# Cross attention: the values made in token layout, without transposes

## The reference

```python
def cross_attention(xn, mem_n, w_q, w_kv, w_o):
    q = (xn @ w_q).reshape(b, s, X_HEADS, X_HEAD_DIM)        # 4 heads of 256
    kv = mem_n @ w_kv
    k = kv[..., :X_HEADS * X_HEAD_DIM].reshape(b, -1, X_HEADS, X_HEAD_DIM)
    v = kv[..., X_HEADS * X_HEAD_DIM:].reshape(b, -1, X_HEADS, X_HEAD_DIM)
    logits = jnp.einsum('bshd,bmhd->bhsm', q, k).astype(jnp.float32) * X_HEAD_DIM ** -0.5
    p = jax.nn.softmax(logits, axis=-1)
    o = jnp.einsum('bhsm,bmhd->bshd', p.astype(v.dtype), v).reshape(b, s, X_HEADS * X_HEAD_DIM)
    return o @ w_o
```

## Time and profile before

| what | value |
|---|---|
| median of three runs | 1918.83 us (1918.15 to 1919.11) |
| profiled execution | 1919.41 us, its span 1917.6 us |
| PE busy | 1893.5 us, 99% of the span |
| POOL busy | 1393.7 us, 73% |
| DVE busy | 943.0 us, 49% |
| ACT busy | 546.1 us, 28% |

### The profile page before, as it was taken

The page is one execution under the profiler, slowest core; times in us unless marked ns, Lnnn a source line. Parts: engine busy times, 40 slices in busy tenths (PEclk is TensorE's granted clock), DMA queues, the critical chain, the costliest instruction groups (busy, mean ns, idle before and its releaser), DMA issues.

```text
span 1917.6 us, 23896 instructions
## 1 busy us (share of the span) xinstructions
PE 1893.5 (99%) x8875; PEld 1564.7 (82%) x8875; DVE 943.0 (49%) x1500; ACT 546.1 (28%) x1093; POOL 1393.7 (73%) x1646
## 2 busy tenths in 40 slices
PE   9999999999999999999999999999999999999997
PEld 7777788888888888888888888888799888888886
DVE  5888788752442212135776664333744643122124
ACT  5666644431120102022345551111322311010012
POOL 6555479998887777778644657777898777777773
PEclk9999999999999999999999999999999999999999
DMA  5222123333333333333322323332433233333321
GB/s 169 78 77 69 48 80 94 96 110 114 95 99 99 94 95 97 99 99 89 87 56 67 88 67 94 99 99 86 126 111 110 81 98 99 99 99 96 92 83 60
DMA packets 341319, 177.43 MB, mean 93 GB/s; under 512 B 14470, under 2 KB 338220, under 8 KB 341205
## 3 DMA queue, kind: packets, MB, share of 16 engines
q1 hardware_dynamic: 338978, 173.14, 31.5%
q10 hardware_dynamic: 2226, 2.76, 0.6%
HBM read 173.75 MB, written 2.13 MB: 92 GB/s over the span
## 4 chain that ended last, share of the span: by engine, by line
PE 93%; DVE 4%; ACT 2%; issue 1%; DVEq 0%; POOL 0%; POOLq 0%; ACTq 0%
PE bank L678 27%; PE bank L680 27%; PE bank L682 27%; PE bank L814 2%; PE bank L766 1%; PE bank L1050 1%; PE bank L1051 1%; PE bank L1052 1%; DVE fQS L1808 1%; PE bank L746 1%; PE bank L792 1%; PE bank L1116 1%; PE bank L1136 1%; PE bank L777 1%; PE bank L862 0%
## 5 line engine op out<-in xcount | busy, mean ns | idle before, releaser
L617 POOL TENSOR_TENSOR WL<-RAW,WH 128x256 fp32r<-128x256 f32 (+2 forms) x1276 | 1031.2, 838 | 29.2
L611 POOL TENSOR_SCALAR WH<-RAW 128x1024 fp32r<-128x1024 f32 (+3 forms) x331 | 354.6, 1071 | 465.0 <-PE bank L682 413.7
L678 PE MATMUL bank<-HH,WH 128*128 128x512 f32 x1560 | 619.0, 397 | 0.5 <-DVE HL L1754 0.5
L682 PE MATMUL bank<-HH,WL 128*128 128x512 f32 x1560 | 615.4, 394 | 0.0
L680 PE MATMUL bank<-HL,WH 128*128 128x512 f32 x1560 | 610.3, 391 | 0.0
L678 PEld LDWEIGHTS bank<-HH,WH 128*128 128x128 f32 x1560 | 293.3, 188 | 60.6 <-issue 6.3
L682 PEld LDWEIGHTS bank<-HH,WL 128*128 128x128 f32 x1560 | 293.0, 188 | 59.4 <-issue 1.9
L680 PEld LDWEIGHTS bank<-HL,WH 128*128 128x128 f32 x1560 | 293.3, 188 | 58.2 <-issue 3.1
L2012 DVE TENSOR_TENSOR X<-X,bank 128x512 f32<-128x512 f32 x80 | 55.0, 687 | 234.1 <-PE bank L682 234.1
L678 PE MATMUL bank<-UH,WH 128*128 128x512 f32 x256 | 99.6, 389 | 0.0
L680 PE MATMUL bank<-UL,WH 128*128 128x512 f32 x256 | 99.6, 389 | 0.0
(11 more groups left out here) (408 smaller groups left out, 2996.8 us busy)
## 6 DMA issues: line engine op xcount, KB each, us to landing
RAW<-in_w_in SPq DMA_DIRECT2D x107, 512.0 KB, 3.6
RAW<-in_w_up SPq DMA_DIRECT2D x32, 512.0 KB, 3.9
RAW<-in_w_down SPq DMA_DIRECT2D x32, 512.0 KB, 3.9
RAW<-in_w_ffn_gate SPq DMA_DIRECT2D x22, 512.0 KB, 3.7
RAW<-in_w_ffn_up SPq DMA_DIRECT2D x22, 512.0 KB, 3.7
RAW<-in_w_xkv SPq DMA_DIRECT2D x16, 512.0 KB, 3.8
RAW<-in_w_ffn_down SPq DMA_DIRECT2D x16, 512.0 KB, 3.9
RAW<-in_w_proj_attn SPq DMA_DIRECT2D x8, 512.0 KB, 3.9
```

Of the source, the lines that this page charges most:

```text
L611: nc.gpsimd.tensor_scalar(WH[:, s, 0:k, :], RAW[:, s, 0:k, :], 1.0, 1.0, ALU.mult, ALU.mult).then_inc(S_[f"hi_made{s}"], 1)
L617: nc.gpsimd.tensor_tensor(WL[:, s, own_tiles, :], RAW[:, s, own_tiles, :], WH[:, s, own_tiles, :].bitcast(F32), ALU.subtract).then_inc(S_[ ...
L678: mm(psum[s][:, 0:n], WH[:, s, k, :], hi(k), start=(k == 0), stop=False)
L682: last = mm(psum[s][:, 0:n], WL[:, s, k, :], hi(k), start=False, stop=(k == tiles - 1))
```

## The change

The values are made with memory tokens on the partitions at once. The memory is the stationary operand (a block of 128 features by 128 tokens), and 256 weight columns of a head move. A unit of the values is now 512 rows by 256 columns, in the same slot and of the same size; both units of a head add into one bank, two blocks of tokens side by side. The transposes and `XV` go. The norm of a token is then one number per partition: two further products with one column give the sums of squares per partition (`RMEM`), ACT takes their root and DVE the reciprocal, and ACT and DVE multiply by it where they make the halves. The bank of a head's values stays taken until then.

```diff
-        XQ, XK, XV = sb("XQ", [P, 2, S]), sb("XK", [P, 2, MEM]), sb("XV", [P, 2, MEM])
+        XQ, XK = sb("XQ", [P, 2, S]), sb("XK", [P, 2, MEM])
...
+        def of_pair(tile, s):
+            return tile[:, s, :, :].rearrange("p (k c) n -> p k (c n)", c=2)
...
+            def load_pair(name, it, j, src):
+                s, c = units.use(name, it, j)
+                sp.wait_ge(S_[f"unit_cut{s}"], 4 * c - 4)
+                sp.dma_start(of_pair(RAW, s), src.rearrange("(k p) n -> p k n", p=P)).then_inc(S_[f"landed{s}"], 16)
...
-                for j in range(4):
-                    load("cross", h, 2 + j, cols(w["w_xkv_2"], h * 2 * P + (D * (j // 2) + P * (j % 2))))
+                for j in range(2):
+                    load("cross", h, 2 + j, cols(w["w_xkv_2"], h * 2 * P + P * j))
+                for j in range(2):
+                    load_pair("cross", h, 4 + j, w["w_xkv_2"][bass.ds(j * D // 2, D // 2), bass.ds(D + h * 2 * P, 2 * P)])
...
-            mm(OUTB[:, 0:MEM], ones[:], ACCM[:], start=True, stop=True).then_inc(once("mem_stat")[0], 1)
+            mm(OUTB[:, 0:MEM], ones[:], ACCM[:], start=True, stop=True)
+            for mb in range(MEM // P):
+                last = mm(OUTB[:, MEM + mb:MEM + mb + 1], ACCM[:, mb * P:(mb + 1) * P], ones[:, 0:1],
+                          start=True, stop=True)
+            last.then_inc(once("mem_stat")[0], 1)
...
-            for j in range(4):
+            def mem_values(h):
+                bank_slot, bank_use = units.use("cross", h, 5)
+                bank = psum[bank_slot]
+                pe.wait_ge(S_[f"taken{bank_slot}"], bank_use - 1)
+                for half in range(2):
+                    s, c = units.use("cross", h, 4 + half)
+                    for k in range(4):
+                        pe.wait_ge(S_[f"unit_cut{s}"], 4 * c - 3 + k)
+                        for mb in range(MEM // P):
+                            for v, weight in ((0, WH), (0, WL), (1, WH)):
+                                last = mm(bank[:, mb * 2 * P:(mb + 1) * 2 * P],
+                                          MEMC[v][:, 4 * half + k, mb * P:(mb + 1) * P], of_pair(weight, s)[:, k, :],
+                                          start=(half == k == mb == v == 0 and weight is WH),
+                                          stop=(half == 1 and k == 3 and v == 1), skip_group_check=True)
+                                if k == 3 and mb == 1 and v == 1:
+                                    last.then_inc(S_[f"product{s}"], 1)
+                                yield
+
+            for j in range(2):
                 run(from_mem(0, 2 + j))
-
-            def cross_values(h):
...
+            run(mem_values(0))
...
                     run(steps, scores_fill[i])
-                    if i == 0:
-                        cross_values(h)
...
-                pe.wait_ge(S_["x_v_hi"], h + 1)
-                pe.wait_ge(S_["x_v_lo"], h + 1)
+                for j in (4, 5):
+                    s, c = units.use("cross", h, j)
+                    pe.wait_ge(S_[f"taken{s}"], c)
+                pe.wait_ge(S_["x_out_lo"], 2 * h + 2)
...
-                              *[from_mem(h + 1, 2 + j) for j in range(4)])
+                              *[from_mem(h + 1, 2 + j) for j in range(2)], mem_values(h + 1))
...
+            A(RMEM[:, 0, :], OUTB[:, MEM:MEM + MEM // P], ACT.Sqrt, bias=EPSC[:], scale=1.0 / D
+              ).then_inc(once("mem_std")[0], 1)
...
                     if i == 0:
-                        act.wait_ge(S_["x_vt"], h + 1)
-                        A(XVC[0][:], OUTB[:].rearrange("p (m e) -> p m e", m=2), ACT.Copy).then_inc(S_["x_v_hi"], 1)
+                        act.wait_ge(S_["x_rstd"], 1)
+                        s, c = units.use("cross", h, 5)
+                        act.wait_ge(S_[f"product{s}"], c)
+                        for mb in range(2):
+                            A(XVC[0][:, mb, :], psum[s][:, mb * 2 * P:(mb + 1) * 2 * P], ACT.Copy,
+                              scale=RMEM[:, 1, mb:mb + 1]).then_inc(S_["x_v_hi"], 1)
...
+            V.reciprocal(RMEM[:, 1, :], RMEM[:, 0, :]).then_inc(S_["x_rstd"], 1)
             own.link(V.reciprocal(RSTDM[:], STDM[:]))
...
                     if i == 1:
-                        dve.wait_ge(S_["x_v_hi"], h + 1)
-                        V.tensor_tensor(XVC[1][:], OUTB[:].rearrange("p (m e) -> p m e", m=2), XVC[0][:].bitcast(F32),
-                                        ALU.subtract).then_inc(S_["x_v_lo"], 1)
+                        dve.wait_ge(S_["x_v_hi"], 2 * h + 2)
+                        bank, _c = units.use("cross", h, 5)
+                        for mb in range(2):
+                            s, c = units.use("cross", h, 4 + mb)
+                            V.scalar_tensor_tensor(XVC[1][:, mb, :], psum[bank][:, mb * 2 * P:(mb + 1) * 2 * P],
+                                                   RMEM[:, 1, mb:mb + 1], XVC[0][:, mb, :].bitcast(F32),
+                                                   ALU.mult, ALU.subtract).then_inc(S_[f"taken{s}"], 1)
...
-                if not last:
-                    cross_take(h + 1, "v")
```

More of the change, by code:

```diff
@@ L243, in program @@
         LOGT = sb("LOGT", [P, 8, 8])
-        sb("pad_small", [P, 16])
+        RMEM = sb("RMEM", [P, 2, MEM // P])
+        sb("pad_small", [P, 12])
         column, n = {}, 0
@@ L1085, in from_mem @@
                 return product("cross", h, j, lambda k: MEMC[0][:, k, :], lambda k: MEMC[1][:, k, :], n=MEM)
-            for j in range(4):
-                run(from_mem(0, 2 + j))
-            def cross_values(h):
[L1092 to L1101, removed]
+            def mem_values(h):
[16 more added lines that the diff above has]
+            for j in range(2):
+                run(from_mem(0, 2 + j))
+            run(mem_values(0))
             def cross(h, steps, scores_fill, turn_fill):
@@ L1585, in _ @@
             act.wait_ge(*once("mem_stat"))
-            A(STDM[:], OUTB[:, 0:MEM], ACT.Sqrt, bias=EPSC[:], scale=1.0 / D).then_inc(once("mem_std")[0], 1)
+            A(STDM[:], OUTB[:, 0:MEM], ACT.Sqrt, bias=EPSC[:], scale=1.0 / D)
+            A(RMEM[:, 0, :], OUTB[:, MEM:MEM + MEM // P], ACT.Sqrt, bias=EPSC[:], scale=1.0 / D
+              ).then_inc(once("mem_std")[0], 1)
             act.preload_act_table(ACT.Exp)
@@ L2311, in cross_take @@
                         else:
-                            unit, dst = (2 + j, XK) if kind == "k" else (4 + j, XV)
-                            take("cross", h, unit, lambda bank: V.tensor_tensor(
-                                dst[:, j, :], bank[:, 0:MEM], RSTDM[:], ALU.mult))
+                            take("cross", h, 2 + j, lambda bank: V.tensor_tensor(
+                                XK[:, j, :], bank[:, 0:MEM], RSTDM[:], ALU.mult))
             def cross_lo(h):
@@ L2325, in _ @@
             cross_lo(0)
-            cross_take(0, "v")
+            dve.wait_ge(S_["x_rstd"], 1)
             def cross(h, last):
```

## The result

The changed kernel takes 1933.64 us (1933.07 to 1934.61) against 1918.93 us before (the 1918.83 of three runs with a fourth one added): a ratio of 1.0078, 95% interval 1.0061 to 1.0095. It is slower by 14.7 us; 1917.5 us, faster by 1.3, was forecast. The profiled execution has a span of 1932.8 us, 15.2 us longer than before.

A forecast was written before the change was run, and what follows sets the result against it. PE was taken to bound the kernel, busy 1893.5 of 1917.6 us. Transposes removed (-1.76) plus norm products added (+0.48) gave -1.28 us, so 1918.83 became 1917.5 us (forecast's chance 0.75), range 1915.8 to 1919.7.

The forecast's parts named there:

- that all else stays as it is: Whole kernel: if the span moves over 3.8 us without the stage's forecast signs changing, the cause lies outside the stage.
- no new wait of PE: Cross attention, 1390 to 1505 us: no new PE wait of more than 0.1 us.
- Rival 2: Value products: moving weights space the 192 matmuls wider than 0.12 us; at 0.15 us, 1923.3 us; chance 0.07.
- Value products: Cross attention heads: again 48 matmuls per head, 0.12 us apart with weights moving, price nothing.
- Transposes: Cross attention heads: four value transposes per head removed, 0.44 us a block, 1.76 us saved over four heads.
- Norm in token layout: Memory norm, behind the ACCM product: two added one-column products, 4 instructions on PE's path, 0.48 us.
- Halving: Cross attention values: halving moved, DVE gives back 0.56 us a head, ACT pays 0.33; 0.464 and 0.478 us per instruction.
- rival 3: Last head's probability transposes: PE idles for the DVE pair, saving given back, 1918.5 us or 1919.0; chance 0.13.
- Loads: Weight loads: same number and order, value rows 1 KB instead of 512 B, landing changes hidden, price nothing.
- The sum: Whole kernel: -1.76 + 0.48 = -1.28 us, bounds -2.40 and -0.49, passed to the end as PE's own work.

The follow-up runs named there:

- realigned kernel: The changed kernel with pad_small at 8 floats instead of 12, so every tile behind it starts where it did before the change: 1917.23 us, ratio to before 0.9993.

## Why the prediction was wrong

**The step that failed** is the one that the prediction left to its last sentence, "that all else stays as it is". The change was taken apart into value products, transposes, norm, halving, waits and loads, and each was priced; the two lines of the diff that declare `RMEM` and shorten `pad_small` were not priced at all. Their bytes add up to what stood there, their places in memory do not: the 16 bytes take 32. What these two lines cost is the difference between the changed kernel and the realigned one, 1933.64 against 1917.23 us, 16.4 us; the 32 bytes alone, in the kernel before, cost 15.6. The span moved by more than 3.8 us while the stage showed what was forecast or less (a head 28.77 us, the value products 0.118 us apart, no new wait of PE), and, as that sentence says, the cause lay outside the stage. Rival 2, the wrong side that was named, is wrong as well: its loss would have been in the value stream, spaced 0.147 us or more.

**The other steps held.** They are read from the realigned kernel, which is the change without the shift. Its chain around the second head, up to the start of the third (start, us on the chain, what):

```profile
1430.71 0.72 PE bank L1140 x6
1433.27 0.71 PE bank L1140 x6
...
1453.92 5.76 PE bank L1115 x48
1459.68 0.72 PE bank L1140 x6
```

- *Value products, nothing.* 48 in 5.76 us, 0.120 us apart with the weights moving, as forecast.
- *Transposes, -1.76 us.* The head takes 28.97 us (1430.71 to 1459.68); 28.96 was forecast from 29.40.
- *Norm in token layout, +0.48 us.* From the product on `ACCM` to the second product behind it, the one on `HL`, are 0.77 us before and 1.22 us in the realigned kernel, +0.45; to the first one, on `HH`, 0.35 and 0.90, +0.55. Before:

```profile
1384.82 0.70 PE L1079 MATMUL bank<-ACCM,ones 128*128 128x256 f32 x2 [0.68 <-DVE ACCM L2297]
1385.17 0.58 PE L678 MATMUL bank<-HH,WH 128*128 128x512 f32 x1
1385.59 0.40 PE L680 MATMUL bank<-HL,WH 128*128 128x512 f32 x1
```

  Realigned:

```profile
1383.58 0.70 PE L1092 MATMUL bank<-ACCM,ones 128*128 128x256 f32 x2 [0.68 <-DVE ACCM L2327]
1384.12 0.50 PE L1094 MATMUL bank<-ones,ACCM 128*128 128x1 f32 x4
1384.48 0.49 PE L691 MATMUL bank<-HH,WH 128*128 128x512 f32 x1
1384.80 0.40 PE L693 MATMUL bank<-HL,WH 128*128 128x512 f32 x1
```

- *Halving.* The forms cost what their neighbours in the earlier trace rows said, 470 ns on ACT and 475 on DVE (groups by line and shape, realigned):

```profile
L2368 DVE SCALAR_TENSOR_TENSOR XVL<-bank,RMEM,XVH 128x256 fp32r<-128x256 f32 x8 | 3.5, 475 | 0.0
L1638 ACT ACTIVATE XVH<-bank,RMEM 128x256 fp32r<-128x256 f32 x8 | 3.3, 470 | 0.0
```

- *The tight place of rival 3.* In the last head the last row of probabilities ends at 1496.34 and the transposes start at 1496.85, 0.51 us later, against the 0.49 that the prediction left; no wait came of it (realigned, DVE and PE):

```profile
1495.70 0.64 DVE L2392 TENSOR_SCALAR XPR<-XPR,RS 128x256 f32<-128x256 f32 x1
...
1496.85 0.60 PE L1147 MATMUL bank<-ident,XPR 128*128 128x128 f32 x4
```

- *Loads.* The loads of keys and values, half of them now with rows of 1 KB, land in 3.7 us instead of 3.8, and POOL still waits for PE alone in this stage.
- *The sum, -1.28 us.* 1918.58 to 1917.23 is -1.35 us. The times by themselves can't tell this from nothing (the interval reaches 1.0002); the trace can, term by term.

What speaks of a shift is in the whole diff, in a kernel that carries two named pads. The trace of before could not have given its price: there all the distances between streamed tiles and weights are multiples of 512 bytes, so no row shows another case.

**What stays open** is the mechanism. The runs show that a matmul of 512 columns gets longer by the distance between the tile that it streams and the weights of its product: on average by 3 ns (64 bytes) to 7 ns (96 bytes), and by nothing at 256. The cost does not follow the size of the shift, as 32 bytes cost twice what 64 do. Why the distance matters, no run shows. The Trainium skill (TensorE: Matmul & The Clock Gate, Part 2: What happens when you issue a matmul) says that PE has two independent read ports, so that loading the next weights takes nothing from the running matmul. By that one would expect the place of the weights to be free, and it is not: with the weights moved by 32 bytes and all else at its old place modulo 512, 1957.75 against 1918.78 us. The Trainium skill (SBUF — State Buffer, Who interferes with whom) says that PE never waits on anyone. As far as POOL, DVE and ACT go, the traces agree: the loss is the same where these are idle, 234 ns from start to start against 227.

## What to carry to other kernels

A diff that declares, drops or resizes any tile moves every tile behind it: work out where the large ones land, with the rounding of the small ones (here to 32 bytes), before pricing the instructions. When a result surprises, look first at groups that the change does not touch: one that takes 395 ns instead of 389 for the same instruction points to a cause outside the changed lines. And try a change with the tiles put back before judging it; here it was worth 1.3 us by the trace, too little for the times to show, and the shift that came with it cost twelve times that.

## What the runs showed of the hardware that was not expected

Time of the kernel before, by the distance that its streamed tiles (except `HH` and `HL`) are moved against the weights: 32 bytes +15.6 us, 64 bytes +7.8, 96 bytes +17.8, 128 bytes +15.8, 256 bytes 0. By 32 bytes the other way (the front tiles moved): +15.6 us. By 32 bytes for all streamed tiles at once (the weights moved): +39.0 us, 2%. By 32 bytes for streamed tiles and weights together: no difference. Products of 256 columns behave differently: moved by 32 bytes, those on the memory became shorter, a head's 48 values 5.69 instead of 5.76 us.
